# Two more places in a weight ring, and gate and up biases split into three bfloat16 parts

## The reference: what is computed

```
logits = xt @ w_router + b_router              # 256 tokens, 32 experts
top_vals, top_idx = top_k(logits, 4); gates = softmax(top_vals)
# per expert e, for its tokens xb:
gt = minimum(xb @ w_gate[e] + b_gate[e], 7)
up = clip(xb @ w_up[e] + b_up[e], -7, 7)
hdn = (up + 1) * (gt * sigmoid(1.702 * gt))
out[tokens of e] += gate * (hdn @ w_down[e] + b_down[e])
```

## Time and profile before

| | |
|---|---|
| median of 3 runs | 1791.12 us (1790.63 to 1792.64) |
| the profiled execution, its own time | 1790.87 us |
| its span | 1789.0 us |
| PE busy | 95% of the span |
| DMA, mean over the span | 366 GB/s |
| granted TensorE clock, mean | 0.997 |

### The profile page before, as it was taken

The page is one execution under the profiler, slowest core; times in us unless marked ns, Lnnn a source line. Parts: engine busy times, 40 slices in busy tenths (PEclk is TensorE's granted clock), DMA queues, the critical chain, the costliest instruction groups (busy, mean ns, idle before and its releaser), DMA issues.

```text
span 1789.0 us, 28857 instructions
## 1 busy us (share of the span) xinstructions
PE 1707.8 (95%) x12156; PEld 768.8 (43%) x12156; DVE 391.3 (22%) x943; ACT 284.7 (16%) x559; POOL 28.0 (2%) x107
## 2 busy tenths in 40 slices
PE   8999999999999999999999999999999999988887
PEld 4543333333333333333333335756446665555554
DVE  3542111121212112121111122443331111111111
ACT  2311111111111101000000112130011222211111
POOL 3020000000000000000000000000000000000000
PEclk9999999999999999999999999999999999999999
DMA  9649999999999997999999996433278999999997
GB/s 312 215 155 430 428 429 428 428 428 429 428 429 429 428 428 313 426 428 428 428 428 429 429 408 213 175 102 122 106 285 371 429 429 429 428 428 429 428 429 307
DMA packets 73528, 655.27 MB, mean 366 GB/s; under 512 B 13216, under 2 KB 16048, under 8 KB 36240
## 3 DMA queue, kind: packets, MB, share of 16 engines
q1 hardware_dynamic: 70736, 651.91, 87.8%
q0 software_dynamic: 528, 1.98, 0.3%
q10 hardware_dynamic: 2224, 0.79, 0.2%
HBM read 653.62 MB, written 1.05 MB: 366 GB/s over the span
## 4 chain that ended last, share of the span: by engine, by line
PE 68%; DMA 29%; DVE 2%; ACT 1%; issue 0%; SPq 0%; ACTq 0%; DVEq 0%
PE ps L1654 27%; DMA ring<-in_w_up 16%; DMA scr<-in_w_up_experts 13%; PE ps L1687 7%; PE ps L1959 6%; PE ps L2019 6%; PE ps L1478 3%; PE ps L1639 3%; PE ps L1736 2%; PE ps L1546 2%; PE ps L1714 1%; PE ps L1648 1%; PE ps L1663 1%; PE ps L1801 1%; PE ps L1742 1%; PE ps L1702 1%
## 5 line engine op out<-in xcount | busy, mean ns | idle before, releaser
L1654 PE MATMUL ps<-ring,Z 128*64 128x512 f32 x3072 | 678.6, 595 | 14.1 <-DMA ring<-in_w_up 13.5
L1654 PEld LDWEIGHTS ps<-ring,Z 128*64 128x64 f32 x3072 | 213.4, 137 | 450.9 <-issue 414.8
L1687 PE MATMUL ps<-ring,Z 128*32 128x128 f32 x2752 | 166.0, 409 | 16.1 <-DMA ring<-in_w_up_experts 9.9
L1687 PEld LDWEIGHTS ps<-ring,Z 128*32 128x32 f32 x2752 | 105.0, 127 | 73.2 <-DMA ring<-in_w_up_experts 15.4
L2019 PE MATMUL ps<-ring,xT 128*128 128x512 f32 (+1 forms) x256 | 105.7, 567 | 0.0
L1639 PE MATMUL ps<-h,Z 128*32 128x256 f32 (+1 forms) x776 | 99.8, 468 | 0.4 <-DVE Z L1026 0.3
L1056 DVE TENSOR_SCALAR Z<-ps 128x512 f32<-128x512 f32 x32 | 22.1, 692 | 355.8 <-PE ps L1654 355.8
L630 ACT COPY Z<-ps 128x256 f32<-128x256 f32 (+1 forms) x63 | 30.0, 477 | 303.5 <-PE ps L1654 229.6
L621 ACT COPY Z<-ps 128x256 f32<-128x256 f32 x64 | 23.8, 372 | 318.3 <-PE ps L1695 318.3
L1058 DVE TENSOR_SCALAR Z<-ps 128x512 f32<-128x512 f32 x32 | 22.1, 692 | 228.9 <-PE ps L1654 228.9
L1068 DVE TENSOR_TENSOR Z<-Z,ps 128x128 f32<-128x128 f32 x32 | 9.2, 287 | 287.2 <-ACT Z L617 287.2
(11 more groups left out here) (430 smaller groups left out, 1340.7 us busy)
## 6 DMA issues: line engine op xcount, KB each, us to landing
ring<-in_w_gate SPq DMA_DIRECT2D x64, 2048.0 KB, 19.0
ring<-in_w_up SPq DMA_DIRECT2D x64, 2048.0 KB, 22.0
ring<-in_w_down SPq DMA_DIRECT2D x64, 2048.0 KB, 19.2
ring<-in_w_gate_experts SPq DMA_DIRECT2D x22, 2048.0 KB, 34.2
ring<-in_w_up_experts SPq DMA_DIRECT2D x21, 2048.0 KB, 34.6
ring<-in_w_down_experts SPq DMA_DIRECT2D x21, 2048.0 KB, 34.1
ring<-in_w_in SPq DMA_DIRECT2D x12, 2048.0 KB, 12.6
scr<-in_w_up_experts SPq DMA_DIRECT2D x11, 2048.0 KB, 36.6
```

What stands on the lines that cost most here:

```text
L1654: last = pe.matmul(dst[CAP * j:CAP * (j + 1)], lhsT, rhs(j), start=start, stop=True, skip_group_check=True)
L1687: last = pe.matmul(bank(4)[CAP2 * t:CAP2 * (t + 1), P * s:P * (s + 1)], picked[:, chunk * CAP2:(chunk + 1) * CAP2], v[:, c, t:512:4], star ...
```

## The change

The first block's ring gets eight places: the six of `ring` and the two 2 MB stretches of `scr` that the second block already uses (`homes` 6 and 7). An expert's pieces go round in them (`place`, `HOME[0]`), so that the pattern repeats after four experts, and PE's and SP's loops hold four experts (`QUAD = 4`). One counter `used1` takes the place of the six `slot_free`. The gaps with other work move to where the loops of four end (`BIAS_AT` 6 to 9, `EMB_AT` 12 to 13). What stood in `scr` during the experts moves to `xT`, `xs` and `Z`. The gate and up biases become three bfloat16 parts (a value, the rest, the rest of the rest) in partitions 0 to 95, with zeros in 96 to 127, so that one bfloat16 matmul over 128 partitions gives their sum. POOL makes them.

```diff
-        HOME = (range(SLOTS), (4, 5, 0, 1, 6, 7, 8, 2, 3))
-        TRIPLE = 3
+        HOME = ((0, 1, 2, 3, 6, 7, 4, 5), (4, 5, 0, 1, 6, 7, 8, 2, 3))
+        QUAD, TRIPLE = 4, 3
+        def place(k, u, i):
+            return HOME[k][(PER[k] * u + i) % len(HOME[k])]
...
             def fill_first():
-                for s, dst, src in expert_loads(0, E - 1, 0):
-                    if s < 4:
-                        sp.wait_ge(sem("proj"), 2 * s + 2)
+                for i, home, src in expert_loads(0, E - 1, 0):
+                    if home < 4:
+                        sp.wait_ge(sem("proj"), 2 * home + 2)
                     else:
-                        sp.wait_ge(sem("out1"), 2 * s - 6)
...
-                for s, dst, src in expert_loads(0, E - 2, 0):
-                    sp.wait_ge(free[s], 1)
+                        sp.wait_ge(sem("mix_ready"), 4)
+                    sp.dma_start(homes[home], src).then_inc(full[home], 16)
+                for i, home, src in expert_loads(0, E - 2, 1):
+                    if i < 2:
+                        sp.wait_ge(sem("out1"), 2 * home - 6)
+                    else:
+                        sp.wait_ge(sem("used1"), i - 1)
...
+                def fill_listed(p, u):
+                    e = sp.value_load(lst[0:1, ds(p + ORDER, 1)], min_val=0, max_val=E - 1)
+                    for i, home, src in expert_loads(0, e, u):
+                        sp.wait_ge(sem("used1"), p * 6 + (i - 7))
+                        sp.dma_start(homes[home], src).then_inc(full[home], 16)
...
@@ POOL, ahead of the wait for mix_ready
+            pool.wait_ge(sem("qk_turned"), 4)
+            pool.wait_ge(sem("pooled"), 1)
+            for part in range(3):
+                for i, name in enumerate(("b_gate", "b_up")):
+                    pool.dma_start(bias_rest[E * part:E * (part + 1), D * i:D * (i + 1)], w[name][0]).then_inc(sem("router_loaded"), 16)
+            pool.memset(bias_gu[3 * E:4 * E, :], 0.0)
+            pool.wait_ge(sem("router_loaded"), 16 * 6)
+            for part in range(3):
+                rows96 = slice(0, E * (3 - part))
+                last = pool.tensor_copy(bias_gu[rows96, :], bias_rest[rows96, :])
+                if part < 2:
+                    step(last)
+                    rows96 = slice(0, E * (2 - part))
+                    step(pool.tensor_tensor(bias_rest[rows96, :], bias_rest[rows96, :], bias_gu[rows96, :], ALU.subtract))
+            last.then_inc(sem("consts"), 1)
+            pool.wait_ge(sem("consts"), 2)
...
                 def gate_up_bias(q, p):
...
-                    for r in range(4):
-                        rows32 = slice(E * r, E * (r + 1))
-                        pe.matmul(bank(4 + r // 2)[CAP * (r % 2):CAP * (r % 2 + 1)], pick_bias[rows32, :], bias_gu[rows32, :],
-                                  start=True, stop=True, skip_group_check=True)
+                    for i in range(2):
+                        halves(bank(4 + i), pick_bias[:, :], lambda j: bias_gu[:, D * i + 512 * j:D * i + 512 * (j + 1)], True)
...
+                    def four(n):
+                        for u in range(1, QUAD):
+                            chained(n * QUAD + u, n, u, n * QUAD + (u - 1))
+                        chained(n * QUAD + QUAD, n + 1, 0, n * QUAD + (QUAD - 1))
```

More of the change, by code:

```diff
@@ L217, in expert_loads @@
             if k == 0:
[L218 to L222, removed]
-                v = src(DOWNS[0], "a (j p c) n -> p j (a c n)", j=2)
[L224 to L231, removed]
+                pieces = []
+                for name in (GATES[0], UPS[0]):
+                    v = src(name, "a (p c) n -> p (a c n)")
+                    pieces += [v[:, 0:SLOT], v[:, SLOT:2 * SLOT]]
+                v = src(DOWNS[0], "a (j p c) n -> p j (a c n)", j=2)
+                pieces += [v[:, 0, :], v[:, 1, :]]
+            else:
+                pieces = [src(GATES[1], "a (p c) n -> p (a c n)"), src(UPS[1], "a (p c) n -> p (a c n)"),
+                          src(DOWNS[1], "a (p j) n -> p (a j n)")]
+            return [(i, place(k, u, i), piece) for i, piece in enumerate(pieces)]
         LAST = ({"gate": 1, "up": 3, "down": 5}, {"gate_up": 1, "down": 2})
@@ L365, in fill_second @@
+                for p in (2, 3):
+                    fill_listed(p, p)
+                with sp.Fori(1, E // QUAD) as n:
+                    for u in range(QUAD):
+                        fill_listed(n * QUAD + u, u)
             def fill_second():
                 for u in range(TRIPLE):
-                    for s, dst, src in expert_loads(1, u, PER[1] * u):
-                        home = HOME[1][s]
+                    for i, home, src in expert_loads(1, u, u):
                         if home < SLOTS:
@@ L404, in _ @@
             fill_leftover(0)
+            last_in_first = {HOME[0][i % 8]: i for i in range(6 * E - 8, 6 * E)}
             for i, ((src, c, n), _) in enumerate(middle):
@@ L1274, in embed @@
                 dve.wait_ge(sem("ple_gate"), b + 1)
-                step(tt(half(emb, b), half(emb, b), half(xs, b), ALU.mult))
-                tt(half(h, b), half(h, b), half(emb, b), ALU.add).then_inc(sem("embedded"), 1)
+                e = emb[b // 2][:, 512 * (b % 2):512 * (b % 2 + 1)]
+                step(tt(e, e, half(xs, b), ALU.mult))
+                tt(half(h, b), half(h, b), e, ALU.add).then_inc(sem("embedded"), 1)
             for b in range(3):
@@ L1689, in gate_up @@
                                                  start=c == 0, stop=True, skip_group_check=True)
-                        last.then_inc(freed(s), 1)
+                        last.then_inc(freed, 1)
                 def back_turn(q, p):
@@ L1705, in hid_turn, with down @@
                     last.then_inc(done_by(q, "pe", "hid"), 1)
-                def down(q, p, s0, filled, freed):
+                def down(q, p, u, filled, freed):
                     after(pe, k, q, "act", "hid", p)
@@ L1715, in down @@
                                                  v[:, j, T * t:T * (t + 1)], start=j == 0, stop=True, skip_group_check=True)
-                        last.then_inc(freed(2), 1)
+                        last.then_inc(freed, 1)
                         return
@@ L1791, in chained, with x_gate_up @@
                         turn_rows(q, p + 1)
-                        down(q, p, *main(p, 0))
-                    def x_gate_up(s, chunks=range(4)):
-                        v, out = slot(s, 4, 1024), 256 * (s // 2)
-                        for c in chunks:
+                        down(q, p, *main(n, u))
+                    def x_gate_up(s):
+                        v, out = slot(place(0, EXTRA_AT % QUAD, s), 4, 1024), 256 * (s // 2)
+                        for c in range(4):
                             cc = 4 * (s % 2) + c
```

275 lines of the change are left out of this document (129 added, 146 removed).

## The result

The changed kernel takes 1775.22 us (median of four, 1773.82 to 1776.34), the kernel before 1791.88 us (1790.63 to 1793.01): a ratio of 0.9907, 95% interval 0.989 to 0.9924. That is 16.7 us less, where 20.8 were forecast. The profiled execution took 1774.97 us, its span 1773.1.

A forecast was written before the change was run, and what follows sets the result against it. The DMA's stream of expert pieces, not PE's speed, was taken to bound the first block's experts. 1790.87 - 9.8 - 12.0 + 1.0 = 1770.1, with 0.25 us for the median 1770.3 us; range 1766.5 to 1780.

The forecast's parts named there:

- Two more places: Start of first block's experts: two more pieces load while the DMA is idle, 184 behind in place of 186, 9.8 us less.
- The idle DMA: Extra expert: eight places hold PE's lead of 22.9 us, so the DMA's idle time goes to zero, 12.0 us less.
- with little to spare: Extra expert: the lead of 22.9 us was to stay just below the 23.3 us that eight places hold.
- rival 4: First block's expert loops: PE stalls at jumps of long bodies, slower overall if each costs 5.8 us; chance 0.05.
- The biases: Each expert's bias pass: bfloat16 pairs at once, 0.55 to 0.6 us saved, off the path but keeping the lead below 23.3.
- rival 2: Experts: bias pass isn't cheaper, 4.1 us idle at the extra expert, gain 17.7, 1774.4 us; chance 0.12.
- POOL beside DVE: Front: POOL's five splitting instructions beside DVE's softmax cost 1 us, bounded from 0 to 9.6.
- one small row: Front, kernel before: DVE's L841 took 0.23 us at 8.71 during POOL's selects, read as not held.
- rival 1: Front: DVE and POOL take turns, up to 9.6 us later, 1772 to 1779, most likely 1776 us; chance 0.27.
- the near end: Front: POOL's cost to DVE taken as 1 us, near the low end of 0 to 9.6.

The follow-up runs named there:

- e4: Changed kernel, ring still eight, but the second expert's first two gate pieces also wait for the first freed place: 1784.69 us, ratio 0.996.
- e5: Changed kernel with the ring back at six places and one expert a body in PE's loops in place of four: 1791.0 us, ratio 0.9996.
- e2: Kernel before with gaps at experts 9 and 13 and four experts a body in PE's loops, ring still six: 1793.26 us, ratio 1.0006.
- e1: Kernel before with only the bias and embedding gaps moved from experts 6 and 12 to 9 and 13: 1793.84 us, ratio 1.0010.
- e9: Changed kernel run once more, unaltered, on the chip shared with e10 and e11: 1774.95 us, ratio 0.9911.
- e8: Changed kernel with POOL's five splitting instructions moved ahead of the six loads, run on zeros, biases left out of the result: 1779.87 us, ratio 0.9926.
- e7: Changed kernel without POOL's five splitting instructions, loads kept, biases left out of the result: 1772.32 us, ratio 0.9886.
- e11: Changed kernel with each expert's bias pass issued four times: 1793.1 us, ratio 1.0009.
- e3: Changed kernel with the ring back at six places, three-part bfloat16 biases and four-expert bodies kept: 1792.32 us, ratio 1.0002.
- e6: Changed kernel with each expert's four bfloat16 bias matmuls issued twice: 1773.64 us, ratio 0.9896.
- e10: Changed kernel with bias loads and POOL's splitting moved earlier, plus one copy to bias_gu, all of the reference computed: 1773.03 us, ratio 0.9895.

## Why the prediction came out as it did

**Two more places, -9.8: right.** e4 measures 9.7 on the stage.

**The idle DMA, -12.0: right in kind; the late landings were left out.** The dip is gone. Between waits the kernel before lost 12.95 us. By the queues' rate from 640 to 760, 384 GB/s, 120 x (1 - 384/428.5) = 12.5 of them are idle, near my 12.0. The other 0.5 is late landing there too: the last part is 2.2 us behind the first ahead of the idle and 2.7 us some pieces later, after steps of 5.12 and 5.97 us that stand behind fetches at 719.9 and 747.2. Against the 12.95 stands what I had put at nothing: the fetches of the long bodies. In the changed kernel the 30 pieces to 617.49 took 148.41 us in place of 146.85, the 60 to 912.73 took 295.24 in place of 293.70, 3.1 us together. -9.79 - 12.95 + 3.10 = -19.64 is the stage's -19.66. The first stretch is shown by e5. In the second, behind the extra expert, the two late steps stand behind fetches as listed there, and 0.4 us is idle that is left: SP found no free place from 665.8 to 681.09, and the queues moved 385, 401 and 418 GB/s in the three windows of 2 us from 681 on. So the ring was full for a moment, and "with little to spare" was right. Short bodies in a ring of eight, which would show how much of the 3.1 us can be had back, weren't run. In my text, rival 4 asked for fetches at PE, where they cost nothing (e2); their cost lay in the DMA's stream. The Trainium skill, "Runtime: NRT & Kernel Launch", section "Instruction fetch mechanics", has the refill in 16 KiB blocks by a DMA queue and calls its cost mostly hidden; the fetch rows have that size, and for PE it is hidden here, for a stream that fills all sixteen engines it is not.

**The biases: the pass as forecast (0.43 to 0.45 us, pairs at once), what it protects mis-sized.** I had 4.1 us of idle return with a dearer pass; with 0.86 us none did. The step that failed, in rival 2, is the lead at expert 17: late landings take 1.5 us of it, so that 11.7 - 5 x (29.37 - 27.20) - 1.5 is nothing, and PE does wait there. What the extra stretch gives is also less: 685.30 - 634.74 = 50.6 us, not the 51.2 of 53.3 - 0.6 - 1.5. In the ring of eight the cheaper pass earns next to nothing, in a ring of six up to 5.6 us (e5 against e1). A float32 pass of 1.01 us in the ring of eight wasn't run.

**POOL beside DVE, +1.0: the size held, the place didn't.** The forecast had the chain beside the softmax at 73 to 78 and took a value near one small row. The loads landed 17 us after their issue at 63.3 (I had allowed 2.3 to 9.2), the chain ran from 80.84 to 95.77, past the softmax, and met L839 to L956, where 3.4 us of PE's cover took most of 4.6 and 4.9 us (the changed kernel and e9): 1.2 to 1.4 us are left. Had the loads landed as allowed, e8 says that rival 1 would have cost 4.6. The forecast was right by luck in this term. The reason that I gave for the near end was a misreading. The small row is L841 of the kernel before (L866 in the changed kernel and e9, L859 in e7; another L841 is meant above). POOL's row at 8.29 is two selects. The first ended at 8.91, and L841 right behind it, at 8.71 + 0.23 = 8.94:

```profile
8.29 0.62 POOL L433 TENSOR_SCALAR_AFFINE_SELECT Z<-Z 128x512 f32<-128x512 f32 x1
```

The same instruction took 0.16 us in e9, where it started at 8.84. In e7 it started at 9.02 and waited for the end of the second select:

```profile
8.29 1.31 POOL L445 TENSOR_SCALAR_AFFINE_SELECT Z<-Z 128x512 f32<-128x512 f32 x2
```

```profile
9.02 0.60 DVE L859 TENSOR_SCALAR st<-st 128x2 f32<-128x2 f32 x1
```

8.29 + 1.31 = 9.60, 9.02 + 0.60 = 9.62. So the small row, read by its ends, spoke for rival 1. The Trainium skill, "SBUF — State Buffer", section "Who interferes with whom", names what can be held (an instruction with two SBUF inputs, tensor_scalar in a two-port mode) and what never is (reductions). The rows above agree, the two at 8.29 too; in which mode the small instructions ran they don't show.

**The front's other +0.3**: 0.77 us by which this execution was later already at L839, less 0.45 for the cheaper first pass.

**Behind the stage, +2.26**: 1.70 of it is L1983's 8.83 in place of 7.13 us at a granted clock of 0.89. PE had idled for 1.34 and 0.78 us just before it, and so it had in e9, where the clock stayed at 1.00. Of the experiments only e11 has the dip at that place (8.66 us); elsewhere it comes in others too (0.91 over 20 us at 380 in e3 and e4, at 1140 in e1). The other 0.56 lies in the scatter of this part: 740.6 to 744.6 us in all kernels but e11, e9 with 743.33 and a dip at 1130 among them, and 740.6 to 741.8 in those without a dip but at the very end (before, e5, e6, e7). So 16.7 by the medians compares with 20.8: 3.1 for the late landings less 0.95 for the idle, some 0.3 for POOL, and the rest, about 1.6, is of the size of such dips.

## What to carry to other kernels

Where a stream of transfers sets a stage, count its pieces behind the first freed buffer and its idle time; a buffer filled while the queue is idle anyway is worth one piece's time there (e4), and a cheaper computation only what it keeps the stream from idling. Between two waits of the consumer, idle and late landings are measured together; the queues' rate gives the idle alone, and the difference is what to look for in the landings. Work put on POOL "beside" DVE has a place in time set by its loads: look where its inputs land under load, and put it where DVE has no two-input or scalar instructions, as e10 does. Whether a small instruction was held is read from where it ends, not from how short it is.

## What the hardware showed beyond that

- Instruction fetches of 16 KB each delayed the landing of whole pieces by 1.5 us over 30 pieces, with 428 GB/s moved either way; most fetches delayed nothing.
- A DVE instruction of 128x8 stood 2.67 us behind a POOL subtraction, one of 128x4 3.48 us, one of 128x8 1.81 us behind a POOL memset; a POOL cast in turn stood 1.1 us behind DVE.
- Of six POOL loads of 128 KB the last landed 17 us after its issue while the ring's big pieces ran.
- POOL's two-input instruction of 2048 columns took 4.06 to 4.93 us, its cast 1.88, where one-input instructions at 1.28 ns a column had made me expect 2.6.
- TensorE's granted clock fell to 0.91 over single windows of 20 us at changing places, up to four in an execution; where one fell on L1983 it cost 1.5 to 1.7 us.
